# Two transformer blocks on one core: the first input product in two halves of K, its shift and scale summed half by half

## The reference, cut to what matters

```python
mod = jax.nn.silu(c) @ w_ada[l] + b_ada[l]            # (1, 2048) @ (2048, 6*2048)
sh1, sc1, ga1, sh2, sc2, ga2 = jnp.split(mod, 6, axis=-1)
h = rms_norm(x, g_norm1) * (1 + sc1) + sh1             # x: 256 positions x 2048
qa, ka, va, oa, gates, qb, kb, vb = jnp.split(h @ w_in[l], IN_SPLITS, axis=-1)
...                                                    # mlstm (a) and neighbourhood attention (b)
x = x + ga1 * (concat(h_a, h_b) @ w_out)
h = rms_norm(x, g_norm2) * (1 + sc2) + sh2
x = x + ga2 * conv_glu(h, ...)
...                                                    # a second block, no w_ada in it
```

## Time and profile before

| | us |
|---|---|
| median of 3 runs (lowest, highest) | 2710.62 (2708.59, 2711.7) |
| profiled execution, its own time | 2712.82 |
| its span | 2711.0 |
| TensorE busy | 2583.1 (95%) |
| VectorE busy | 1651.8 (61%) |
| ScalarE busy | 1205.1 (44%) |
| GpSimd busy | 209.2 (8%) |
| DMA moved | 567.38 MB, mean 209 GB/s |

### The profile page before, as it was taken

One profiled execution on the slowest core, in us unless ns is written; L12 is line 12 of the kernel. 1 busy time (PEld: TensorE's weight loads), 2 busy tenths in 40 slices (PEclk: granted clock), 3 DMA queues, 4 the chain that ended last, 5 costly groups with the idle time before them and its releaser, 6 DMA issues.

```text
span 2711.0 us, 33373 instructions
## 1 busy us (share of the span) xinstructions
PE 2583.1 (95%) x11934; PEld 2132.5 (79%) x11934; DVE 1651.8 (61%) x1839; ACT 1205.1 (44%) x1518; POOL 209.2 (8%) x255
## 2 busy tenths in 40 slices
PE   0699999999999999999999999999999999999998
PEld 0587887878888888888888867778888888888886
DVE  7887777867676756544454475656554545454454
ACT  1143445534444444344454455654454444444443
POOL 2111114110000000000110030202000000000000
PEclk9999999999999999999999999999999999999999
DMA  9798777847767655555566545355556565665554
GB/s 394 288 358 281 250 251 237 275 159 259 239 222 242 198 188 183 181 189 191 190 203 192 190 125 155 117 184 196 186 187 193 186 193 185 191 188 189 194 193 146
DMA packets 273148, 567.38 MB, mean 209 GB/s; under 512 B 23829, under 2 KB 24189, under 8 KB 272541
## 3 DMA queue, kind: packets, MB, share of 16 engines
q1 hardware_dynamic: 247264, 494.99, 55.3%
q0 software_dynamic: 18960, 69.40, 7.6%
q10 hardware_dynamic: 6828, 1.72, 0.5%
HBM read 563.94 MB, written 2.10 MB: 209 GB/s over the span
## 4 chain that ended last, share of the span: by engine, by line
PE 89%; DVE 5%; issue 2%; DMA 1%; ACT 1%; POOL 1%; SPq 1%; ACTq 0%; DVEq 0%; POOLq 0%
PE gp L1173 28%; PE gp L1175 28%; PE gp L1174 27%; DVE ada_sum L1698 2%; DVE w_lo L1591 1%; PE tp L1404 1%; DMA ada_ring<-in_w_ada_dram 1%; DMA proj<-in_w_ada_dram 1%; PE tp L1196 1%; PE tp L1225 1%; PE tp L1216 0%; ACTq L818 0%; PE tp L1571 0%; PE tp L1315 0%; PE tp L1449 0%
## 5 line engine op out<-in xcount | busy, mean ns | idle before, releaser
L1591 DVE TENSOR_TENSOR w_lo<-raw,w_hi 128x1024 fp32r<-128x1024 f32 x872 | 1071.4, 1231 | 872.2 <-ACT w_hi L684 869.7
L684 ACT CAST w_hi<-raw 128x1024 fp32r<-128x1024 f32 x872 | 913.1, 1051 | 1108.6 <-PE gp L1175 1055.7
L1173 PE MATMUL gp<-w_hi,h_hi 128*128 128x512 f32 x2656 | 1048.7, 395 | 4.2 <-DVE w_lo L1591 2.6
L1175 PE MATMUL gp<-w_hi,h_lo 128*128 128x512 f32 x2656 | 1036.6, 390 | 0.0
L1174 PE MATMUL gp<-w_lo,h_hi 128*128 128x512 f32 x2656 | 1036.1, 390 | 0.0
L1173 PEld LDWEIGHTS gp<-w_hi,h_hi 128*128 128x128 f32 x2656 | 499.8, 188 | 110.6 <-issue 5.6
L1175 PEld LDWEIGHTS gp<-w_hi,h_lo 128*128 128x128 f32 x2656 | 499.6, 188 | 105.1
L1174 PEld LDWEIGHTS gp<-w_lo,h_hi 128*128 128x128 f32 x2656 | 500.0, 188 | 101.0 <-issue 0.2
L1173 PE MATMUL gp<-w_hi,a_hi 128*128 128x512 f32 x704 | 275.0, 391 | 0.0
L1175 PE MATMUL gp<-w_hi,a_lo 128*128 128x512 f32 x704 | 274.2, 389 | 0.0
L1174 PE MATMUL gp<-w_lo,a_hi 128*128 128x512 f32 x704 | 274.1, 389 | 0.0
(11 more groups left out here) (275 smaller groups left out, 1366.8 us busy)
## 6 DMA issues: line engine op xcount, KB each, us to landing
raw<-in_w_in_dram SPq DMA_DIRECT2D x248, 512.0 KB, 3.7
raw<-in_w_up_dram SPq DMA_DIRECT2D x176, 512.0 KB, 4.3
raw<-in_w_ffn_in_dram SPq DMA_DIRECT2D x176, 512.0 KB, 3.9
ada_ring<-in_w_ada_dram POOLq DMA_DIRECT2D x128, 512.0 KB, 5.5
raw<-in_w_down_dram SPq DMA_DIRECT2D x88, 512.0 KB, 3.7
raw<-in_w_ffn_down_dram SPq DMA_DIRECT2D x88, 512.0 KB, 4.5
proj<-in_w_ada_dram SPq DMA_DIRECT2D x64, 512.0 KB, 7.7
raw<-in_w_out_dram SPq DMA_DIRECT2D x64, 512.0 KB, 4.6
```

The lines of the kernel that those rows point to most:

```text
L684: nc.scalar.copy(w_hi[:, s], raw[:, s]).then_inc(hi_ready, 1)
L1173: mm(o, hi[:, kt0 + kt, ps], w_hi[:, s, k, :], start=n == 0, stop=False)
L1175: last = mm(o, lo[:, kt0 + kt, ps], w_hi[:, s, k, :], start=False, stop=n == g.kts - 1)
L1591: V.tensor_tensor(w_lo[:, s], raw[:, s], w_hi[:, s].bitcast(F32), ALU.subtract).then_inc(lo_ready, 1)
```

## The change

`g_in_a` becomes `g_in_a0` and `g_in_a1`: 6 chunks of 4 blocks each over the first 8 K-tiles, then the same 6 chunks over the last 8. So 48 blocks as before, but the first 24 need only half of `h`, and so only 8 x 128 = 1024 columns of `sh1` and of `sc1`.

- SP loads the pieces by halves: 16 K-tiles x (1 of the scale, 1 of the shift) = 32 pieces ahead of the product, 32 during `g_in_a0`, in an order written out (`halves_adds` says how many after which block). Four slots for the scale, four for the shift.
- Of the shift's first half, TensorE sums 14 of 16 K-tiles itself: for each, 8 products with 128 columns of the piece as the stationary operand and silu(c) as the one moving column, accumulated in PSUM as columns (`shift_product`). DVE weighs the scale's 16 and the shift's last 2, and all 32 of the second half.
- `column_sums` replaces `sum_rows`, the row copy and the transpose: 8 + 8 products with one moving column of ones; the result stands in columns. The biases come in by a product with the identity (`shift_bias`). `mod_half` makes 8 columns of `mod` each.
- h = x*scale + shift moves from DVE to ACT (`high_affine`). Pairs 0 to 3 before the first block; pairs 4 to 7 at the start of `g_in_a1`.
- ACT drains both halves of the positions: `g_in_a0` to `proj`, `g_in_a1` to a buffer `partial`. GpSimd adds the two (12 additions of 128x512).
- The 96 pieces of `ga1`, `sh2`, `sc2` are spread anew: 20 in `g_in_a1`, 41 in `g_in_b`, 11 in `g_in_o`, 24 in `g_out`. `K1` is 10 instead of 12. Buffers and semaphores are renamed to fit; `hf` and the gate weights move to `gate2`.

```diff
+            def load_ada(n, which):
+                half, k = n // DT, n % DT
+                if n >= 4:
+                    if which:
+                        sp.wait_ge(sc_summed, n - 3)
+                    else:
+                        sp.wait_ge(*shift_used(n - 4))
...
+            for n in range(DT):
+                load_ada(n, 1)
+                load_ada(n, 0)
...
+                if n == 6:
+                    prime(g_in_a0)
+            for j in range(g_in_a0.nb):
+                load(g_in_a0, 0, 1, j)
+            q = 2 * DT
+            for b in range(-1, g_in_a0.chunks * g_in_a0.nb):
+                if b >= 4:
...
+                    load(g, c_ // 2, c_ % 2, j)
+                for _ in range(8 + 4 if b < 0 else halves_adds(b)):
+                    if q < 4 * DT:
+                        load_ada(q // 2, 1 - q % 2)
+                        q += 1
...
+        def halves_adds(b):
+
+            if b < 4:
+                return 1 if b < 2 else 0
+            return (2 if b % 2 == 0 else 1) if b <= 20 else 0
...
+            def shift_product(n):
+
+                pe.wait_ge(ada1_landed[n % 4], 16 * (n // 4 + 1))
+                for q in range(HK1):
+                    last = mm(column(q), ada1[1][:, n % 4, q * P:(q + 1) * P], c_act[:, n:n + 1],
+                              start=False, stop=False)
+                last.then_inc(sh_used, 1)
...
+            column_sums(0)
             pe.wait_ge(mod_ready, 1)
-            transpose_x(0, range(4), 0)
-            stream(g_in_a, h_hi, h_lo, 0, h_pairs(HB_NORM0), each=rest_of_x(0, 0))
+            transpose_x(0, (3,), 0)
+
+            def in_a0_each(i, e, j, first):
+                b = (2 * i + e) * g_in_a0.nb + j
+                if b == 5:
+                    transpose_x(0, (4, 5, 6), 0)
+                    pe.wait_ge(h_full, 4)
+                    shift_bias(1)
+                if b == g_in_a0.chunks * g_in_a0.nb - 2:
+                    column_sums(1)
...
+            mod_half(0)
+            for kp in range(4):
+                low_half(kp)
+                weigh(*late.pop(0))
+            for b in range(g_in_a0.chunks * g_in_a0.nb):
+                if b >= RING:
+                    c_ = b // g_in_a0.nb
+                    split(g_in_a0, c_ // 2, c_ % 2, b % g_in_a0.nb)
+                for _ in range(halves_adds(b)):
+                    weigh(*late.pop(0))
...
+            n0 = AR
+            for c_ in range(g_in_a1.chunks):
+                n1 = min(4 * c_ + 7, IN_A_ADA + AR)
+                ada_cols(range(n0, n1))
+                n0 = n1
+                for t in range(ST):
+                    pool.wait_ge(drained[t], g_in_a1.chunk0 + c_ + 1)
+                    o = proj[:, t, c_ * CW:(c_ + 1) * CW]
+                    nc.gpsimd.tensor_tensor(o, o, partial(c_ % 2, t), ALU.add).then_inc(in_sum, 1)
```

More of the change, by code:

```diff
@@ L1280, in mlstm @@
                         pe.wait_ge(gc_ready, 1)
-                        for t in range(ST):
-                            pe.wait_ge(drained[t], g_in_b.chunk0)
+                        pe.wait_ge(in_sum, ST * g_in_a1.chunks)
                     for q in range(2):
@@ L1749, in _, with weigh @@
-            stream(g_in_a, drain_proj(g_in_a, proj, 0), each=ada2(0), nxt=g_in_b, ahead=RING + 1)
+            def weigh(n, which):
+                half, k = n // DT, n % DT
+                dve.wait_ge(ada1_landed[4 * which + n % 4], 16 * (n // 4 + 1))
+                ring, col = ada1[1 - which][:, n % 4, :], c_act[:, k:k + 1]
+                dst = ada_sum[:, (0 if which else 2) + half, :]
+                done = sc_summed if which else sh_summed
+                before = n if which else n - SH_PE
+                if k == 0 or before == 0:
+                    ins = V.tensor_scalar(dst, ring, col, None, ALU.mult)
+                else:
+                    dve.wait_ge(done, before)
+                    ins = V.scalar_tensor_tensor(dst, ring, col, dst, ALU.mult, ALU.add)
+                ins.then_inc(done, 1)
@@ new lines, in _ @@
+            dve.wait_ge(silu_ready, 1)
+            for n in range(DT):
+                weigh(n, 1)
+                if n == 8:
+                    dve.wait_ge(vec_ready, 1)
+                    gfin = vcol[:, 0, VC["gfin"]:VC["gfin"] + DT]
+                    link(V.tensor_tensor(gfin, gfin, vcol[:, 0, VC["mixg"]:VC["mixg"] + DT], ALU.mult))
+                    dve.wait_ge(ident_ready, 1)
+                    norm_stats(0)
+                    make_diag(0)
+                if 9 <= n < 13:
+                    prime(g_in_a0, (n - 9,))
+                if not shift_by_pe(n):
+                    weigh(n, 0)
@@ new lines, in _ @@
+            late = [(q // 2, 1 - q % 2) for q in range(2 * DT, 4 * DT)]
+            mod_half(0)
[8 more added lines that the diff above has]
+                    weigh(*late.pop(0))
+            prime(g_in_a1, (0, 1))
@@ L1751, in at @@
+            stream(g_in_a1, nothing, each=in_a1_each, nxt=g_in_b, unrolled=True)
             def at(g, part):
```

355 lines of the change are left out of this document (219 added, 136 removed).

## The result

The changed kernel took **2690.70 us** (median of 5 runs, 2687.45 to 2701.56) where the kernel before, run between, took 2710.62: ratio **0.9933** over all runs, 95% interval 0.9921 to 0.9945. So it is faster, by 20 us where 40 were forecast, and outside the range given. In a second session it took 2698.26 (2691.56 to 2699.49), ratio 0.9943 (0.9930 to 0.9957); that it has such a spread, and the kernel before has not (2707.35 to 2713.28 over all sessions), is part of the story.

The account below looks back on a forecast made before the run. Bound: TensorE's own pace once running, and ahead of it a 107 us prologue bound by loading. Gain 42.3 - 2.0 - 0.5 = 39.8 us off 2712.82, giving 2673.0, less 2.2 against the median: 2670.8; range 2661 to 2683.

Parts of the forecast that it names:

- A: Rival for g_in_a0: loading slower in the mix, 363 GB/s, last blocks late by 8 to 9 us, 2679; chance 0.2.
- B: Rival for g_in_a1: GpSimd's additions make VectorE the bound, 8 us, 2679; chance 0.1.
- D: Rival for g_in_a0: TensorE's short waits hold the clock at 1.2 GHz, slower than before, 2728; chance 0.03.
- my 0.4: Start of g_in_a0: first 4 us at the low clock cost 1.9 us, all but 0.4 hidden.
- TensorE's 112 one-column products for the shift: Prologue: 1 us per K-tile, hidden behind the 2.5 us that a pair of pieces takes to load.
- 8 products with a column of ones, 0.8: Prologue, after the last weighing: the column sums take 0.8 us of the 4.0 before the first product.
- 59.8: End of prologue: time in us at which the first large product starts, 47.5 us earlier.
- VectorE is the bound of `g_in_a0`: Blocks 4 to 20 of g_in_a0: VectorE needs 5.88 us per two blocks, TensorE 5.43, so TensorE waits.
- The 4.3 us of waits that I had put in: g_in_a0: TensorE's short waits on `w_lo` for VectorE, beginning about block 4, 3 to 5 us in sum.
- Column sums of the second half: g_in_a0, between blocks 22 and 23: 16 one-column products, 1.8 us with the hand-over.
- The gate chain of `g_in_b`: g_in_b: 41 weighings instead of 36 cost 0, up to 3 us if they fall before a wait of TensorE.
- `g_in_o`: 4.2 for 2.0: Start of g_in_o: masks and the load behind them come later, costing 2.0 us, between 0 and 4.

Follow-up runs that it names:

- wide_rows: Changed kernel, TensorE's shift sums made per K-tile by two products with 512 moving columns instead of 8 one-column products; 2690.26 us, ratio 0.9927.
- split_sums: Changed kernel, second half's column sums parted: 8 for the scale ahead of block 21, 8 for the shift ahead of block 22; 2697.65 us.
- shift8: Changed kernel, TensorE sums 8 K-tiles of the first shift instead of 14, VectorE weighs the last 8; 2688.74 us, ratio 0.9927.
- warm: Changed kernel with one idle 512-column product more per K-tile of the shift, result unused; 2711.08 us.
- shift12: Changed kernel, TensorE sums 12 K-tiles of the first shift instead of 14, VectorE weighs the last 4; 2687.73 us, ratio 0.9913.
- masks_late: Changed kernel, the fourth mask's first operation done four times, so GpSimd's load behind the masks is issued later; 2698.18 us.
- after_again: The changed kernel run once more, unaltered, for its spread, in a second session; 2698.26 us.
- together: Changed kernel with wide_rows, split_sums, block 6's weighing in g_in_b moved to block 31, and GpSimd's first load ahead of the fourth mask; 2683.44 us, ratio 0.9896.

## Why the prediction was half right

**What held.** The bound was the prologue, and the loading ahead of the product was halved as forecast: the other half of the pieces, loaded beside `g_in_a0` at 380 and 414 GB/s (80 to 100, 100 to 120 us), made no block late. By its own sign, windows under 390 between 55 and 115, A came true (337 in 60 to 80, 380 in 80 to 100). But its price did not: SP's queue waited for slots that VectorE had not yet freed (9.9 us in one piece, up to the first weighing of the second half at 71.9, and 13.6 of the 20 us from 80 on), so the loading was held back and not slow. `g_in_a1` took 66.45 us where 66.3 was due: VectorE's instructions beside GpSimd's additions take up to 2.4 instead of 1.3, and the room was there (B fell). There was no long low clock in `g_in_a0` (D fell): blocks 0 to 4 took 11.9 instead of 10.9 us. The Trainium skill (TensorE: Matmul & The Clock Gate, Part 1) has it that the low level is the default and sustained activity lifts it; this 1.0 lies between the 1.9 of that rule and my 0.4. In the 24 us of one-column products before, the trace doesn't agree with the rule: TensorE was active without a gap and stayed at the price of the low level.

**The step that failed.** "TensorE's 112 one-column products for the shift (at most 0.12 each by four in 0.50) are 1 us per K-tile, and a pair of pieces takes 2.5 us to load: hidden." They are 3.44 us per K-tile, 3.4 times that, and not hidden. Two errors in one reading: the x4 of the earlier trace rows are four instructions, which is two products, so the row's price per product is 0.25; and it was taken where the clock was high, while here TensorE does almost nothing else for 50 us and has it low. That is 8.15 us by wide_rows, which does the same sum at the other price and changes nothing else of weight. The same miscount stands in "8 products with a column of ones, 0.8": 16 products, 32 instructions, 4.2 us, 3.4 more; the last weighing ended 0.8 later. 8.15 + 3.4 + 0.8 = 12.3, the whole of 72.1 - 59.8.

**The step that came out by luck.** "VectorE is the bound of `g_in_a0`": from block 0 to 21 I had 61.4 us, and it took 61.4. VectorE's pace was right (5.9 us per two blocks, busy without a gap). But TensorE never waited for it and ran at its own pace (2.72 a block from block 8 on). The 4.3 us of waits that I had put in were instead the transposes of pairs 4 to 6 ahead of block 5 (3.2 us), which I had left out of TensorE's work, and the low clock at the start (1.0), which I had all but hidden. They kept TensorE just behind VectorE, whose split of block 21 was ready 0.6 us before it was needed. So the sum is right by two errors; the kernels that started 6 to 8 us earlier lost 1.1 us or less of it up to block 21, and had 0.3 to 2.0 us to spare there.

**Terms mis-sized.** Column sums of the second half: 3.7 for 1.8, and a clock fall behind them, 1.4 (split_sums). The ledger shows only 1.6 of these 3.3 us, because I had put in 1.9 for the hand-over behind block 23, the clock and the queues. The gate chain of `g_in_b`: I had 0, up to 3; it was 2.1 to block 56, of which a later stage returned 0.5. I had named the extra weighings as harmless unless they fall before a wait of TensorE, and didn't look where they fall: one stands between two parts of that chain and costs 1.2. The rest is the chain's later start and a clock that stays low for longer, and its cause is open. `g_in_o`: 4.2 for 2.0, at my upper bound in this trace and beyond it in others. The mechanism was right (the masks and the load behind them come later, VectorE waits for it, TensorE behind it); its size isn't a delay but a race with the bias loads, which I hadn't looked at. The earlier trace rows gave the distance to `g_in_o` (7.7 us), and what else was issued near it was in the trace. The rest of the 20 us is in the runs: the kernel before was profiled in an execution 2.2 above its median, the changed one in one 0.6 below.

## What to carry to other kernels

Price a small instruction from a row of its own count and at the clock at which it will run: here many one-column products kept TensorE busy and its clock low, and the same sum with the wide operand moving cost about half, only because the clock rose with it. When a stage is cut short, what comes behind it meets other transfers: list what every queue issues in the 2 us around each load that someone waits for, and put that load first. A gain that is there at one landmark and gone at a later one is a new wait or a slower stretch between them, and a ledger of one repeated product shows where. When a sum comes out right, look whether its terms did: who waited for whom, and how much lead the other engine had left.

## What the runs showed of the chip

- A plain float32 product stands as two instructions. With 128x128 stationary and one moving column each takes 0.115 us at a granted clock of 1.00 (changed kernel, from 138.92) and 0.22 at 0.50 (shift8, 64 to 68); with one stationary column and 512 moving ones 0.43 and 0.85 (wide_rows, 22.82 on).
- 24 us of one-column products without a gap left the clock low, and 3.7 us of them in a row were followed by its fall in 12 of 13 traces, with TensorE never idle. One 512-column product per K-tile beside them, a third of the time, didn't lift it (warm); 512-column products alone did (wide_rows). The clock column of the windows says 1.00 for the whole start of the changed kernel. But its first record of the clock is at 63.84, just where the transposing instructions go from 0.213 to 0.115 apart; ahead of it I go by the durations.
- A 512 KB load from GpSimd's queue issued 0.7 to 1.9 us behind two loads of 96 KB in packets of 256 bytes (ScalarE's queue) was in use 8.8 to 10.5 us after its issue (shift12, wide_rows, split_sums, masks_late, after_again; together's second load), against 4.0 to 4.5 where it was level with them or ahead and VectorE waited for it; in masks_late the core moved 53 GB/s for 4 us meanwhile. The Trainium skill (DMA: Bandwidth & Descriptors, Why small descriptors are slow (HBM only)) gives an overhead of 27% for packets of 256 bytes; 53 is an eighth of the 415 of an undisturbed stretch, so that overhead alone doesn't account for what the row shows.
- From 20 to 35 us loading ran at 414 to 417 GB/s in twelve of the profiled executions and at 380 to 394 in five (shift8, split_sums, warm, masks_late, together), for no reason that the traces show; in together the last weighing ended 3.8 us later than in wide_rows.
